# Expert rows stored by pick and token through an indirect store, in a one-core hybrid layer with a mixture of experts

## The reference

```
h = x + W_out [ PoolMix(u) ; RMSNorm_head(GLA(q, k, v)) * silu(r) ]
hn = rmsnorm(h, norm_ffn)
g = argmax over 4 groups; the 2 best of the group's 8 experts, with two gates
for each of the two picks k of a token: y_k = (silu(hn @ w_eg[e_k]) * (hn @ w_eu[e_k])) @ w_ed[e_k]
h = h + gate_1 * y_1 + gate_2 * y_2
out = rmsnorm(h, norm_final)
```

## Time and profile before

| | us |
|---|---|
| median of 3 runs | 1151.32 |
| lowest and highest | 1149.84, 1154.34 |
| profiled execution, its time | 1154.0 |
| its span, first to last instruction | 1152.0 |

### The profile page before, as it was taken

One profiled execution on the slowest core, in us unless ns is written; L12 is line 12 of the kernel. 1 busy time (PEld: TensorE's weight loads), 2 busy tenths in 40 slices (PEclk: granted clock), 3 DMA queues, 4 the chain that ended last, 5 costly groups with the idle time before them and its releaser, 6 DMA issues.

```text
span 1152.0 us, 31179 instructions
## 1 busy us (share of the span) xinstructions
PE 1043.7 (91%) x13842; PEld 854.4 (74%) x13842; DVE 424.1 (37%) x920; ACT 242.4 (21%) x506; POOL 90.0 (8%) x128
## 2 busy tenths in 40 slices
PE   5999999999999999975999999999999999999910
PEld 5778787868686877735888889888788787878810
DVE  1426162626354453513532233233132232313338
ACT  2334232332323231210111111111101111110114
POOL 0110101010100101001000000000000000000043
PEclk9999999999999999986999999999999999999965
DMA  8980000000000000373999999999999999999858
GB/s 278 400 261 30 0 18 18 0 18 0 18 0 18 0 18 1 118 305 125 373 384 374 394 385 396 397 413 388 376 403 374 404 377 386 399 376 406 351 191 326
DMA packets 58140, 273.61 MB, mean 237 GB/s; under 512 B 6349, under 2 KB 17293, under 8 KB 49914
## 3 DMA queue, kind: packets, MB, share of 16 engines
q1 hardware_dynamic: 47050, 233.79, 52.9%
q0 software_dynamic: 6176, 22.02, 6.0%
q10 hardware_dynamic: 4880, 17.30, 3.7%
HBM read 242.37 MB, written 30.73 MB: 237 GB/s over the span
## 4 chain that ended last, share of the span: by engine, by line
PE 63%; DMA 23%; DVE 10%; issue 2%; ACT 1%; SPq 0%; POOL 0%; DVEq 0%; POOLq 0%; ACTq 0%
DMA arena<-in_w_eu 21%; PE bank L1345 19%; PE bank L1137 17%; PE bank L1246 11%; PE bank L1356 5%; PE bank L1125 2%; PE bank L1362 2%; DVE er L795 2%; PE bank L1215 2%; DVE arena L1106 1%; DVE arena L1105 1%; DMA arena<-in_w_in 1%; DVE arena L1110 1%; PE bank L1239 1%; PE bank L1233 1%
## 5 line engine op out<-in xcount | busy, mean ns | idle before, releaser
L1137 PEld LDWEIGHTS bank<-xnT,arena 128*128 128x128 f32 x1728 | 197.9, 193 | 11.7 <-issue 7.7
L1137 PE MATMUL bank<-xnT,arena 128*128 128x128 f32 x1728 | 199.1, 276 | 3.5 <-DMA arena<-in_w_in 3.5
L1345 PE MATMUL bank<-xnT,arena 128*64 128x96 f32 x4096 | 177.0, 249 | 11.2 <-DMA arena<-in_w_eu 8.9
L1345 PEld LDWEIGHTS bank<-xnT,arena 128*64 128x64 f32 x4096 | 172.5, 139 | 19.1 <-DMA arena<-in_w_eu 10.3
L1345 PE MATMUL bank<-hnT,arena 128*64 128x96 f32 x4096 | 175.0, 247 | 9.0 <-DMA arena<-in_w_eu 8.6
L1345 PEld LDWEIGHTS bank<-hnT,arena 128*64 128x64 f32 x4096 | 170.1, 137 | 17.5 <-DMA arena<-in_w_eu 10.1
L989 DVE TENSOR_SCALAR mixT<-mixT 128x384 f32<-128x384 f32 x32 | 11.5, 360 | 321.9 <-ACT mixT L666 321.9
L1246 PE MATMUL bank<-arena,mixT 128*128 128x512 f32 x288 | 126.9, 599 | 2.9 <-DVE mixT L836 2.9
L1246 PEld LDWEIGHTS bank<-arena,mixT 128*128 128x128 f32 x288 | 54.6, 192 | 69.4 <-issue 65.7
L1356 PE MATMUL bank<-arena,silu_r 128*32 128x384 f32 x768 | 85.8, 487 | 0.5 <-issue 0.5
L1362 PE MATMUL bank<-arena,osq 128*32 128x256 f32 x384 | 86.1, 380 | 0.0
(11 more groups left out here) (194 smaller groups left out, 1004.6 us busy)
## 6 DMA issues: line engine op xcount, KB each, us to landing
arena<-in_w_eg SPq DMA_DIRECT2D x32, 2048.0 KB
arena<-in_w_eu SPq DMA_DIRECT2D x32, 2048.0 KB, 27.6
arena<-in_w_ed SPq DMA_DIRECT2D x32, 2048.0 KB, 27.6
expert_rows<-zeros SPq DMA_DIRECT2D x1, 8448.0 KB, 57.6
arena<-in_w_in SPq DMA_DIRECT2D x3, 2048.0 KB, 14.7
expert_rows<-kz_v ACTq DMA_DIRECT2D x16, 384.0 KB, 7.1
expert_rows<-hs ACTq DMA_DIRECT2D x16, 384.0 KB, 7.3
hn_rows<-hs ACTq DMA_DIRECT2D x9, 512.0 KB, 2.7
```

What stands on the lines that cost most here:

```text
L1137: last = mm(out, w_in_sb[:, k, a:b], xnT[:, k, :], start=k == 0, stop=k == KD - 1)
L1345: last = mm(out[q * SW:(q + 1) * SW, n * BLOCK:(n + 1) * BLOCK], w[:, k, m * P + q * SW:m * P + (q + 1) * SW], rowsT[b][:, k, :], start=k ...
```

## The change

Results are stored at a row that is named by pick and token, no longer at the expert's place. `hn_dram` gets a second copy of its rows, so that the one index (pick x 1152 + token) serves for reading `hn` and for writing the result. The index table starts from 4096 in place of 0; a filled slot adds its row number less 4096. An unused slot thus names a row out of bounds, and the indirect DMA leaves it out (`oob_is_err=False`), in reading and in writing. The store of an expert's result goes from ScalarE's queue (plain) to GpSimd's (`scatter`, indirect), in program order behind the gather of the expert two further on. The zeros are no longer stored, and `slot_i` is gone. The last stage reads plain blocks of 128 rows through SyncE (64 rows in tile 0); in odd tiles ScalarE multiplies with the root mean square and GpSimd with `g_fin`, in even tiles VectorE does both as before.

```diff
-    hn_dram = nc.dram_tensor("hn_rows", (TILES * P, D), F32, kind="Internal").ap()
-    ys_dram = nc.dram_tensor("expert_rows", (SLOTS, D), F32, kind="Internal").ap()
+    hn_dram = nc.dram_tensor("hn_rows", (PICK_ROWS, D), F32, kind="Internal").ap()
+    y_dram = nc.dram_tensor("pick_rows", (PICK_ROWS, D), F32, kind="Internal").ap()
...
@@ SyncE
-            sp.wait_ge(s["setup_pool"], 5)
-            sp.dma_start(ys_dram[NE * BLOCK:, :].rearrange("(p b) (c n) -> p (b c) n", p=BLOCK, n=ZW),
-                         zeros[:, :].unsqueeze(1).to_broadcast([BLOCK, EXTRA * D // ZW, ZW])).then_inc(s["zeros_stored"], 16)
...
+            for b in range(2):
+                sp.wait_ge(ye_stored[b], 16 * (NE // 2))
             for i in range(TILES):
-                sp.wait_ge(s["out_ready"], i + 1)
+                for k, y in ((0, y1[i]), (1, y2[i])):
+                    at_row = (k * TILES + i) * P
+                    sp.dma_start(y[0:OUT_ROWS[i], :], y_dram[at_row:at_row + OUT_ROWS[i], :]).then_inc(y_in[i], 16)
+            for i in range(TILES):
+                sp.wait_ge(out_ready[i], 1)
...
@@ GpSimd
+            def scatter(t, b, first=False):
+                e = 2 * t + b
+                if not first:
+                    wait_parted(pool, ye_stored[b], 16 * t, s["parted"])
+                nc.gpsimd.tensor_copy(pick_idx[b][:, :], idx_i[:, bass.ds(e, 1)]).then_inc(s["pick_idx_ready"], 1)
+                wait_parted(pool, s["pick_idx_ready"], e + 1, s["parted"])
+                wait_parted(pool, s["ye_ready"], YE_STEPS * (e + 1), s["parted"])
+                nc.gpsimd.indirect_dma_start(y_dram, bass.IndirectOffsetOnAxis(ap=pick_idx[b][:, :], axis=0), ye[b], None,
+                                             bounds_check=PICK_ROWS - 1, oob_is_err=False).then_inc(ye_stored[b], 16)
...
-            with pool.Fori(1, NE // 2) as t:
+            pool.wait_ge(s["pe_eT"], 1)
+            gather(1, 0)
+            pool.wait_ge(s["pe_eT"], 2)
+            gather(1, 1)
+            scatter(0, 0, first=True)
+            scatter(0, 1, first=True)
+            with pool.Fori(2, NE // 2) as t:
                 for b in range(2):
                     wait_parted(pool, s["pe_eT"], 2 * t + b - 1, s["parted"])
                     gather(t, b)
+                    scatter(t - 1, b)
+            for b in range(2):
+                scatter(NE // 2 - 1, b)
...
-            for i in range(TILES):
-                for y, k in ((y1[i], 0), (y2[i], 1)):
-                    nc.gpsimd.indirect_dma_start(y, None, ys_dram,
-                                                 bass.IndirectOffsetOnAxis(ap=slot_i[:, i * PICKS + k:i * PICKS + k + 1], axis=0),
-                                                 bounds_check=SLOTS - 1).then_inc(y_in[i], 16)
+            for i in range(1, TILES, 2):
+                pool.wait_ge(s["scaled_ready"], (i + 1) // 2)
+                nc.gpsimd.tensor_tensor(y2[i], y2[i], g_fin, ALU.mult).then_inc(out_ready[i], 1)
...
@@ ScalarE
-                act.dma_start(hn_dram[bass.ds(j * P, P), :], hs[:, :, :].rearrange("p k n -> p (k n)")).then_inc(s["hn_stored"], 16)
+                for k in range(PICKS):
+                    act.dma_start(hn_dram[bass.ds(k * TILES * P + j * P, P), :], hs[:, :, :].rearrange("p k n -> p (k n)")).then_inc(s["hn_stored"], 16)
...
-                act.wait_ge(s["ye_ready"], YE_STEPS * (e + 1))
-                act.dma_start(ys_dram[bass.ds(e * BLOCK, BLOCK), :], ye[b]).then_inc(ye_stored[b], 16)
...
+                rstd_i = A(fss[0:r, i:i + 1], fss[0:r, i:i + 1], ACT.Exp, scale=-0.5)
+                if i % 2:
+                    final.then(rstd_i)
+                    A(y2[i], y1[i], ACT.Copy, scale=fss[:, i:i + 1]).then_inc(s["scaled_ready"], 1)
+                else:
+                    rstd_i.then_inc(s["frstd_ready"], 1)
...
@@ VectorE
-            V.memset(idx_f[:, :], 0.0).then_inc(s["idx_added"], 1)
+            V.memset(idx_f[:, :], float(NO_ROW)).then_inc(s["idx_added"], 1)
...
-                V.tensor_scalar(M_tok[:, :, :], Mk, token[:, 0:1], None, ALU.mult).then_inc(s["onehot_ready"], 1)
+                V.tensor_tensor(M_tok[:, :, :], Mk, token[:, :].unsqueeze(2).to_broadcast([P, PICKS, NE]), ALU.mult).then_inc(s["onehot_ready"], 1)
...
             for i in range(TILES):
                 combine(i)
-                if i:
+                if i % 2:
                     normalize(i - 1)
             normalize(TILES - 1)
```

More of the change, by code:

```diff
@@ L64 @@
 EXTRA = (PICKS * TOKENS - 1) // BLOCK
-SLOTS = (NE + EXTRA) * BLOCK
+PICK_ROWS = PICKS * TILES * P
+OUT_ROWS = [SAMPLE] + [P] * (TILES - 1)
+NO_ROW = 4096
 BIG = 3.0e38
@@ L182, in build @@
         one_dv = sb("one_dv", [P, P])
-        ZW = 256
-        zeros = sb("zeros", [BLOCK, ZW])
         eps = sb("eps", [P, 1])
@@ L288, in build @@
         rows_idx = [sb(f"rows_idx{b}", [BLOCK, 1], I32) for b in range(2)]
+        pick_idx = [sb(f"pick_idx{b}", [BLOCK, 1], I32) for b in range(2)]
         idx_xf = sb("idx_xf", [BLOCK, EXTRA])
@@ L322, in build @@
         y_in = [sem(f"y_in{i}") for i in range(TILES)]
+        out_ready = [sem(f"out_ready{i}") for i in range(TILES)]
         w_in_v = w_in.rearrange("(p k) n -> p k n", k=KD)
@@ L441, in _ @@
             pool.memset(sB[:, :, :], 0.0).then_inc(s["setup_pool"], 1)
-            pool.memset(zeros[:, :], 0.0).then_inc(s["setup_pool"], 1)
+            pool.memset(sum2[:, :, 0:1], 0.0).then_inc(s["setup_pool"], 1)
             def windows(i, first=False):
@@ L706, in _ @@
                 act.wait_ge(s["fin_ready"], i + 1)
[L707 to L709 removed]
+                r = OUT_ROWS[i]
+                final.then(A(y2[i][0:r, :], y1[i][0:r, :], ACT.Square, scale=D ** -0.5, accum_out=fss[0:r, i:i + 1]))
+                final.then(A(fss[0:r, i:i + 1], fss[0:r, i:i + 1], ACT.Ln, bias=eps[0:r, 0:1]))
+                rstd_i = A(fss[0:r, i:i + 1], fss[0:r, i:i + 1], ACT.Exp, scale=-0.5)
[4 more added lines that the diff above has]
+                    rstd_i.then_inc(s["frstd_ready"], 1)
         @block.vector
@@ L1046, in _, with table @@
             xt = Steps(dve, s["x_tab_dve"])
-            once.then(V.tensor_copy(token[:, :], con("token")))
-            once.then(V.memset(idx_xf[:, :], 0.0))
-            def table(n):
+            once.then(V.tensor_copy(token[:, :], con("pick")))
+            once.then(V.memset(idx_xf[:, :], float(NO_ROW)))
+            def table(n, k):
                 xt.begin(n)
@@ L1070, in _ @@
                 with dve.Fori(0, TILES) as i:
-                    table(2 * i)
-                    table(2 * i + 1)
+                    for k in range(PICKS):
+                        table(PICKS * i + k, k)
                     V.tensor_scalar(token[:, :], token[:, :], float(P), None, ALU.add).then_inc(s["x_dve"], 1)
@@ L1103, in combine @@
             def combine(i):
-                dve.wait_ge(y_in[i], 32)
-                final.then(V.scalar_tensor_tensor(out=y1[i], in0=y1[i], scalar=gate_all[:, i, 0:1], in1=h_all[:, i, :], op0=ALU.mult, op1=ALU.add))
-                V.scalar_tensor_tensor(out=y1[i], in0=y2[i], scalar=gate_all[:, i, 1:2], in1=y1[i], op0=ALU.mult, op1=ALU.add).then_inc(s["fin_ready"], 1)
+                dve.wait_ge(y_in[i], 16 * PICKS)
+                r = OUT_ROWS[i]
+                final.then(V.scalar_tensor_tensor(out=y1[i][0:r, :], in0=y1[i][0:r, :], scalar=gate_all[0:r, i, 0:1], in1=h_all[0:r, i, :],
+                                                  op0=ALU.mult, op1=ALU.add))
+                V.scalar_tensor_tensor(out=y1[i][0:r, :], in0=y2[i][0:r, :], scalar=gate_all[0:r, i, 1:2], in1=y1[i][0:r, :],
+                                       op0=ALU.mult, op1=ALU.add).then_inc(s["fin_ready"], 1)
             def normalize(i):
-                dve.wait_ge(s["frstd_ready"], i + 1)
-                V.scalar_tensor_tensor(out=y2[i], in0=y1[i], scalar=fss[:, i:i + 1], in1=g_fin, op0=ALU.mult, op1=ALU.mult).then_inc(s["out_ready"], 1)
+                dve.wait_ge(s["frstd_ready"], i // 2 + 1)
+                r = OUT_ROWS[i]
+                V.scalar_tensor_tensor(out=y2[i][0:r, :], in0=y1[i][0:r, :], scalar=fss[0:r, i:i + 1], in1=g_fin[0:r, :],
+                                       op0=ALU.mult, op1=ALU.mult).then_inc(out_ready[i], 1)
             dve.wait_ge(s["g_fin_in"], 16)
```

44 lines of the change are left out of this document (18 added, 26 removed).

## The result

The changed kernel is 1.3% slower. Its median is 1166.99 us (1163.41 to 1168.92) beside 1151.76 us for the kernel before on the same chip, a ratio of 1.0127 with the interval 1.0095 to 1.0159. That is 15.2 us more, where 14.8 us less were forecast, and 13 us above the top of the range. The profiled execution spans 1164.9 us, 12.9 more than before.

The account below looks back on a forecast made before the run. The prediction took TensorE, then from about 770 us the DMA engines loading weights, to bound the experts' stage. It subtracted 14 us for skipped rows and 0.8 for the last stage from 1151.3, giving 1136.5 us, range 1129 to 1154.

Parts of the forecast that it names:

- The view of the bottleneck: Late experts' stage: DMA sets the pace, a pair needing 36.6 us of DMA against 33.7 of TensorE.
- Skipped rows: Experts' stage: 1.24 us less a pair if engines share evenly, 17.4 us gained; 10.6 if less even; 14 taken.
- The store from GpSimd's queue: Experts' stage: priced like the plain store, no added cost; 5.5 us at the gather's price kept for the range.
- what waits behind the store: Experts' stage, GpSimd: gathers issued later cost nothing as long as their landing stays below 24 us.
- Head of the last stage: Last stage: VectorE starts 2.6 us earlier, its first step 9.5 us behind the last copy instead of 12.1.
- GpSimd's multiply: Last stage: four multiplies of 1.89 us; three hold VectorE off for that long each, costing 5.7 us.
- Edits put at nothing: Removed zeros, second `hn` store and VectorE's small edits: each expected to change the time by nothing.
- Last stage: End of the kernel: 6.5 us gained by fewer VectorE steps, less 5.7 for GpSimd's multiplies, leaving 0.8 us.
- Rival 1: Experts' stage: neighbouring slots share an engine, so skipping gains nothing; 1150.5 us, or 1144.8 with free multiplies; chance 0.30.
- Rival 2: Experts' stage: neighbouring slots share an engine and the indirect store costs what a gather does; 1158 us, chance 0.14.
- Rival 3: Gathers and stores: a skipped row, or a stand-in for it, is still moved; 1150.5 us, chance 0.08.

Follow-up runs that it names:

- e14: The kernel before with half of the matmuls of `w_eg` and `w_eu` left out, all transfers kept; 1148.78 us, 0.9949 of the kernel before.
- e1: The changed kernel with slots renumbered so unused ones fall on one or two of every six neighbours; 1134.25 us, 0.9828 of the kernel before.
- e18: The changed kernel with half of the matmuls of `w_eg` and `w_eu` left out; 1155.40 us, 1.0001 of the kernel before.
- e16: The kernel before with all rows stored by GpSimd's indirect DMA and half of the matmuls of `w_eg` and `w_eu` left out; 1152.85 us, ratio 0.9992.
- e5: The kernel before with all 96 rows of each expert stored by GpSimd's indirect DMA, nothing skipped; 1161.30 us, 1.0070 of the kernel before.
- e17: The changed kernel with unused slots spread and half of the matmuls of `w_eg` and `w_eu` left out; 1127.67 us, 0.9781 of the kernel before.
- e12: The kernel before with each unused slot reading a row of its own instead of row 0; 1154.82 us, 1.0009 of the kernel before.
- e13: The kernel before with slots renumbered to spread the unused ones, nothing skipped; 1154.36 us, 1.0014 of the kernel before.
- e7: The kernel before with all 96 rows of each expert stored by a plain DMA from GpSimd; 1161.67 us, 1.0062 of the kernel before.
- e6: The kernel before, stores still on ScalarE, with GpSimd waiting for the result copies ahead of the next gather; 1153.01 us, 1.0001 of the kernel before.
- e3: The changed kernel with VectorE normalizing all tiles of the last stage, without GpSimd's multiplies; 1160.61 us, 1.0054 of the kernel before.
- e2: The changed kernel with whole blocks stored plainly from ScalarE's queue, only reads skipped; 1152.26 us, 0.9994 of the kernel before.
- e8: The changed kernel with odd and even slots on the two halves of the ranks; 1145.52 us, 0.9940 of the kernel before.
- e9: The changed kernel with plain whole-block stores from ScalarE, only reads skipped, and unused slots spread; 1133.32 us, 0.9839 of the kernel before.
- e11: The kernel before with later-released gathers and one more store of 96 x 4 bytes per expert from GpSimd; 1318.74 us, 1.1448 of the kernel before.

## Why the prediction was wrong

**The view of the bottleneck was right.** The experts' stage is set by the DMA engines, and what they carry decides. e14 shows it most plainly: with half of the matmuls of `w_eg` and `w_eu` gone the kernel gains 0.5%.

**Skipped rows: the step that failed.** It is "if the 16 engines share what is skipped evenly", from which 14 us followed; the far end that it allowed, 5 of 6 rows on a busiest engine, was not far enough. The gain is real where the clause holds: e1 ends the experts 22.3 us earlier, more than the 17.4 of the sum. Where it doesn't hold, as in the changed kernel, nothing is left (e18 against e16) and the stage got 5.5 us longer still at TensorE's pace (1113.5 against e5's 1108.0). The pair came out at 38.0 us where 35.5 was written. So the experts' term was off by 25 us in three parts: 14 of gain that did not come, 5.5 that packing cost, and 5.5 of the store.

**The size of that term.** The prices by bytes gave 1.24 us a pair; the runs give 1.58 (e16 to e17), and for the reads 1.09 instead of 0.69. A mean price of a queue, its time over its bytes, undervalued a skipped row: the runs give 27% more for reads and writes together and 58% more for reads. Neither the repeated reads of row 0 (e12) nor the numbering (e13) is why.

**The store from GpSimd's queue.** This term of the sum was mis-sized too. The prediction took the plain store's price, so nothing more than before, and kept 5.5 us as the bound for an indirect one. The measured loss is 5.5 us at the end of the experts and 8 in time (e5), so the far end was the better value, but for another reason than the one given: e7 loses as much with a plain store. The part "what waits behind the store" held: gathers land in 13.7 us, far below 24, TensorE never waited for `rows` in a late pair, and e6 shows that the later release costs nothing.

**Head of the last stage.** The first combine was to start 9.5 us behind the last copy; it started 1123.39 - 1113.52 = 9.9 behind it (before 12.3). Right to 0.4 us.

**GpSimd's multiply.** The lock was forecast and is there: a VectorE step of 3.37 us begins beside each of three multiplies of 2.91 us, and in e3, without them, no step is above 1.28. The rule cited from the Trainium skill, page "SBUF — State Buffer", section "SBUF: two separate sides", that such instructions exclude each other, is what the trace shows, now in the direction that no row of before had. The term was small by 3 x (3.37 - 1.28 - 1.89) = 0.6 us; a multiply takes 2.91 us beside VectorE, where 1.89 was worked out. The rest of the last stage's miss, 1.9 us lost for 0.8 gained, is mostly its tail: from the last combine's end, 1155.88 + 1.28 = 1157.16, to the end of the span it is 7.7 us where 6.0 were forecast. Of these 1.7 us, 1.4 lie behind the last step: 1164.9 - 1160.45 = 4.4 us for the store, where e3 has 1159.9 - 1156.87 = 3.0. GpSimd's fourth multiply ends at 1156.45 + 2.91 = 1159.36, so that tile's store goes out just ahead of the last one; that the two delay each other was not tested.

**Edits put at nothing.** The zeros, the second `hn` store and VectorE's small edits moved nothing: the first gather goes out at 528.5 us, before at 528.36 in the chain.

**The sum again.** Experts: +11.0 for -14. Last stage: +1.9 for -0.8. Together 27.7 us of the 30.0 between forecast and measured difference; the other 2.3 lie between the profiled executions and the medians.

**The rivals.** Rival 1 had the mechanism (neighbouring slots share an engine) and 0.30. The Trainium skill, page "DMA: Bandwidth & Descriptors", section "Why a DMA increments its semaphore by 16 and not by 1", gives ⌈partitions/16⌉ partitions to an engine for some direct copies. The trace agrees for the indirect ones here, six neighbours of 96 to an engine, as the seven small packets in the first 57 ns show. Rival 1 took for granted that an engine left idle costs nothing, and gave 1150.5. Rival 2, with 0.14, was the right sign and nearest in time (1158 us for 1167); it added a dear store to rival 1 as the truth did. Its "pairs above 36.6 us" is what the chain shows. What made the range too low is that both rivals were priced at an engine's full load and no further: full engines beside idle ones were taken to be as fast as 16 full ones. Rival 3 (a stand-in for a skipped row is moved) is true in its words, but the stand-in is a packet of 4 bytes, and the row's bytes are gone.

**What is open.** Why the packed form costs time beyond what it fails to gain, and why the store costs 8 us from GpSimd's queue and about half of that with TensorE out of the way. A reading for the first: each load waits until TensorE has released its buffer, so engines that finish early stand idle until the fullest has landed and TensorE has moved on. That engines stand idle is in the packet records: between 780 and 1020 us fewer than 16 packets were in flight for 8.9% of the time in the changed kernel, 3.7% in e2, 2.6% in e8 and 8.0% in e18, and at no time in the kernel before, e1, e5, e7, e9 and e17. But what stood idle in the changed kernel is by this count at least 1.8% of the 16 engines' time, while the window's GB/s is 4.4% below that of e5 (366 and 383), so idle engines are not shown to be the whole. For the store this reading fails, as e5 and e7 have no such idle time and lose 8 us all the same. Why they do was not tested, nor why a spread, skipped read is worth 1.09 us a pair.

## What to carry to other kernels

Before skipping rows in a DMA, ask which of the 16 engines each row belongs to: with the same bytes skipped, the numbering of the slots alone was worth 33 us of 1167. Where the DMA engines pace a stage, count GpSimd's queue as dearer than ScalarE's for a store beside full DMA engines, plain or indirect (8 us for 32 stores of 384 KB here). Work handed to GpSimd to relieve VectorE must be priced by what VectorE loses beside it; here four steps of 1.28 us saved cost three delays of 2.1 us and a later last store.

## What the hardware showed that was not expected

- **Skipping rows of neighbouring slots gives nothing back.** Against e5, which moves all rows from the same queues, the changed kernel gathers and stores 18.1 MB of experts' rows in place of 25.2 (4416 rows for 6144), and its experts still end 5.5 us later, at 366 GB/s in place of 383; with TensorE out of the way the two are level.
- **A skipped row remains a packet of 4 bytes**, some 9 ns in the records, in gathers and in stores.
- **Very small stores beside full DMA engines are dear.** One more of 384 bytes for each of 32 experts, 12 KB in all, cost 53 and 71 us in two executions from ScalarE's queue, 1.7 to 2.2 us an expert, and 166 us from GpSimd's, 5.2 us an expert. The packets are cut differently (96 of 4 bytes, 16 of 24), so this does not compare the queues. The chain of e11 shows the loads stretched; in e6 such pieces are 29 to 32 us:

```profile
1053.36 39.79 DMA arena<-in_w_ed
...
1101.08 40.66 DMA arena<-in_w_ed
```

- **A plain store moved to GpSimd's queue costs 0.6%** (e7, 1.0039 to 1.0086), as much as an indirect one (e5, 1.0053 to 1.0087).
- **27 reads of one row of HBM in each gather cost nothing** against 27 different ones (e12, 0.9993 to 1.0026).
